# A gMLP layer's norm applied behind its projections, gate chains between the small steps of its mixing, and two weight units split earlier at each border

## The chip, the cores and the metric

The kernel runs on one core of a Trainium2 chip. The metric is the device time of one launch in microseconds (us), the median of three runs. Five engines work side by side, each with its own instruction queue: TensorE (PE, with the weight loads shown apart as PEld), VectorE (DVE), ScalarE (ACT), GpSimd (POOL) and SyncE (SP), which here only issues DMAs. An engine waits for another at a semaphore. TensorE's clock is at one of two levels, 2.4 GHz (granted clock 1.00) or 1.2 GHz (0.50).

## The reference, cut to what matters

One inference step of a two-layer decoder for a prompt of 1024 tokens and a group of 8 samples of one token, with width 1024. Layer 0 mixes by two kinds of attention, layer 1 by a chunked gMLP; each mixer is followed by a SwiGLU FFN of width 2816. Only the second mixer's norm and what follows matter here:

```python
def rms_norm(x, g):
    y = xf * lax.rsqrt(jnp.mean(xf * xf, axis=-1, keepdims=True) + NORM_EPS)
    return (y * g).astype(x.dtype)

def chunk_gmlp(h, w_in, g_v, b_v, w_s, b_s, w_out):
    z = jax.nn.gelu(h @ w_in, approximate=False)
    u, v = z[..., :D_C], z[..., D_C:]
    v = layer_norm(v, g_v, b_v)
    return (u * chunk_mix(v, w_s, b_s).astype(u.dtype)) @ w_out, v
```

with `x += mixer(rms_norm(x)); x += swiglu(rms_norm(x))` in every layer. The factor of a token in `rms_norm` is one number for a whole row of `x`, so `(x*g*r) @ w` equals `r * ((x*g) @ w)`. `chunk_mix` multiplies each group of 128 channels by a causal 128x128 matrix over 128 positions.

## The kernel before

**Layout.** The activations lie transposed in SBUF: `xT`, 8 tiles `m` of 128 channels by 1032 tokens (8 samples, then the prompt). Tokens are worked in three blocks `b`: 0 of 392, 1 of 384, 2 of 256. Every product of float32 numbers is made of three products of rounded halves: `x = Xh + Xl`, `w = Wh + Wl`, and `Wh*Xh + Wh*Xl + Wl*Xh` add up in PSUM (`split_products`, line 510; `chain`, line 503). A **chain** is the 24 matmuls that give 128 outputs for one block; of 392, 384 and 256 columns.

**Weights** come as units of 128x1024. SP loads them in order into two raw buffers (`load_unit`), as the splits free them. POOL splits most: `Wh` at line 377, `Wl` at line 380 (`split_unit`, `split_ahead`); ACT can round one (`round_unit`, 389), with POOL making the rest (`remainder_unit`, 398). Six buffers hold split units, so unit n can be split once PE is done with unit n - 6 (`wait_released`).

**A norm** (`norm_*`, lines 426 to 500) has per block: squares on ACT (`sq`, 428), their sum over m on POOL (`acc_sq`, 436), the sum over channels by a matmul with ones on PE (`norm_total`, 443), a square root on ACT (451), a reciprocal on DVE (457), then per m: `hs = xT*gain*acc_sq` on DVE (465), `Xh` rounded from it on ACT (472), `Xl = hs - Xh` on DVE for even m and on POOL for odd m (479).

**The order** of each engine's work is written out by hand, one function per engine and stage:
- An output projection (`narrow_pe`, `residual_dve`, `residual_act`, `residual_pool`) computes 24 chains; DVE adds each to `xT` (1550). The norm of blocks 0 and 1 is made while the later chains run. The next FFN's gate chains follow: this is a **border**, and there are two, at 790 and at 1895 us. `residual_pool` splits the next units with `ahead`.
- An FFN (`ffn_pe`, `ffn_dve`, `ffn_act`, `ffn_pool`) runs 11 steps of 12 gate chains, `hide` (`hf`, 1766; `Hl`, 1768) and 24 down chains of 6 matmuls, added to `xT` at 1777. In the last step of the first FFN (`LAST_STEP`: gates of blocks 0 and 1, down chains of block 0, gates of block 2, down chains of blocks 1 and 2) the gMLP's norm is made between.
- gMLP (`gmlp_pe`, `gmlp_act`, `gmlp_dve`): first the V half, 18 tiles with tokens on the partitions, 24 matmuls of 512 columns each (`wide_products`, 539 to 541), in 6 PSUM banks, freed by ACT's gelu (1968). Then U chains 1 to 6, while ACT and DVE make the layer norm of V (1977 to 2019); three small steps for the 8 samples (transposes 1940, DVE, 16 small matmuls 1944, copies 2036); the mixing of 16 half tiles (1952, DVE 2042); U chains 7 to 24. U's gelu goes from PSUM to `ug` (1997), `y = mixed * ug` on DVE (2065), then `Xh` on ACT (1988), `Xl` on DVE (2052, `low`) for the output projection. The bank of a U chain is free with its gelu.

The gelu of V, before the change:

```python
act.wait_ge(G["v_ps"], q + 1)
act.activation(dst, ps[0:r, q % V_BANKS, :], ACT.Gelu, accum_out=vsum[0:r, tt, c:c + 1]).then_inc(G["v_gelu"], 1)
```

Of the kernel before, what the change touches and what calls it, by code (L numbers as in the profile page):

```python
# [13 lines left out]
P = 128  # L14
# [3 lines left out]
NS = 8  # L18
# [74 lines left out]
def build(nc, a):  # L93
    with ExitStack() as ctx:
# [107 lines left out]
        vst = place("vst", [P, 4, TT])  # L202
        w00 = place("w00", [P, KT])
# [204 lines left out]
        def wl(n):  # L408
            return Wl[n % SPL]


        norm_sem = {k: (sem(f"norm_{k}"), n) for k, n in (
            ("squared", NB * KT), ("summed", NB * KT), ("total", NB), ("root", NB), ("rstd", NB),
            ("scaled", NB * KT), ("high", NB * KT), ("low_dve", NB * KT // 2), ("low_pool", NB * KT // 2))}

        NORMS = [None] + [{k: Counted(x, n * j) for k, (x, n) in norm_sem.items()} for j in range(3)]
# [1167 lines left out]
        def residual_pool(pool, base, order, norm, ahead):  # L1584
# [10 lines left out]
            for b in range(NB):  # L1595
                if b == NB - 1:
                    ahead(base + HALF + SPL)
                    ahead(base + HALF + 1 + SPL)
# [30 lines left out]
        def ffn_pe(pe, f, base, norm, bank_free, after, between):  # L1629
            def step(i, is_last):  # L1630
# [10 lines left out]
                for p, (kind, x, y, half) in enumerate(jobs):  # L1641
# [707 lines left out]
```

## Time and profile before

| | us |
|---|---|
| median of 3 runs (2666.21 to 2667.39) | 2666.43 |
| the profiled execution, its own time | 2663.21 |
| its span, first to last instruction | 2661.4 |
| PE busy | 2580.7 |
| DVE, POOL, ACT busy | 1128.5, 1111.4, 545.6 |
| second FFN border, V tiles, mixing: about | 1895, 1562 to 1675, 1708 to 1730 |

How to read it: all durations come from the one profiled execution, and positions are us from the start of its span. "Idle before, releaser" is what ended an engine's wait. A busy engine is one that has an instruction under way, so an op that is held up while it runs looks long, not idle.

### The profile page before, as it was taken

What the parts mean: (1) busy time and instruction counts of PE and PEld (TensorE: products, weight loads), DVE (VectorE), ACT (ScalarE), POOL (GpSimd) and SP (SyncE); (2) the same over time, 40 slices, a digit from 0 to 9 for tenths busy, and PEclk for the clock granted to TensorE, in tenths of its full rate; (3) what the DMA queues carried; (4) which work ended last, traced back from release to release, by engine and by line L of the source; (5) the groups of instructions that cost most, each with busy time, mean ns of one, the idle gap of its engine ahead of it and who ended that gap; (6) DMA issues with size and microseconds to landing.
All of it is one profiled execution on the core that took longest, in us unless ns stands there. A gap on an engine that the chain in (4) does not pass through costs nothing.

```text
span 2661.4 us, 42811 instructions
## 1 busy us (share of the span) xinstructions
PE 2580.7 (97%) x16377; PEld 2351.9 (88%) x16377; DVE 1128.5 (42%) x2234; ACT 545.6 (21%) x1255; POOL 1111.4 (42%) x713
## 2 busy tenths in 40 slices
PE   7999989999999999999999999999999999999999
PEld 6777756656899999999999977899999999999999
DVE  6636537667344333333333360433733333333333
ACT  5201126666321000000000141321300000000001
POOL 4224115566666443333333363426643333334440
PEclk9999989999999999999999999999999999999999
DMA  5223147767312111111111111102011111111111
GB/s 160 66 78 89 56 130 233 217 204 211 90 32 80 45 43 47 47 41 46 47 47 47 32 40 40 49 21 60 26 60 43 47 47 47 47 47 47 47 32 64
DMA packets 218460, 189.85 MB, mean 71 GB/s; under 512 B 29443, under 2 KB 171523, under 8 KB 217956
## 3 DMA queue, kind: packets, MB, share of 16 engines
q1 hardware_dynamic: 200996, 161.89, 21.0%
q10 hardware_dynamic: 17344, 26.35, 2.7%
q8 instruction: 76, 1.25, 0.2%
q14 instruction: 44, 0.36, 0.0%
HBM read 171.19 MB, written 17.01 MB: 71 GB/s over the span
## 4 chain that ended last, share of the span: by engine, by line
PE 69%; DVE 2%; POOL 2%; ACT 1%; issue 1%; ACTq 0%; POOLq 0%; DVEq 0%
PE ps L506 64%; DVE hs L465 1%; PE ps L539 1%; PE ps L541 1%; PE ps L540 1%; PE ps L1952 1%; ACT ps L1977 1%; POOL acc_sq L436 1%; DVE acc_sq L457 0%; PE ps L1184 0%; POOL Xl L479 0%; DVE Xl L479 0%; PE ps L1165 0%; PE ps L1212 0%; POOL Wl L398 0%
## 5 line engine op out<-in xcount | busy, mean ns | idle before, releaser
L506 PE MATMUL ps<-Xh,Wh 128*128 128x256 f32 (+2 forms) x2712 | 872.5, 322 | 14.1 <-POOL Wl L380 7.3
L506 PE MATMUL ps<-Xl,Wh 128*128 128x256 f32 (+2 forms) x2712 | 867.2, 320 | 0.0
L506 PE MATMUL ps<-Xh,Wl 128*128 128x256 f32 (+2 forms) x2712 | 866.1, 319 | 0.0
L377 POOL TENSOR_TENSOR Wh<-raw,zeros 128x1024 fp32r<-128x1024 f32 x178 | 353.8, 1988 | 1075.0 <-PE ps L506 788.8
L506 PEld LDWEIGHTS ps<-Xh,Wh 128*128 128x128 f32 x2712 | 510.0, 188 | 20.8 <-issue 17.0
L506 PEld LDWEIGHTS ps<-Xl,Wh 128*128 128x128 f32 x2712 | 510.0, 188 | 0.8
L506 PEld LDWEIGHTS ps<-Xh,Wl 128*128 128x128 f32 x2712 | 510.5, 188 | 0.0
L380 POOL TENSOR_TENSOR Wl<-raw,Wh 128x1024 fp32r<-128x1024 f32 x178 | 439.6, 2470 | 14.0
L1768 DVE TENSOR_TENSOR Hl<-hf,Hh 128x392 fp32r<-128x392 f32 (+1 forms) x132 | 180.2, 1365 | 465.9 <-ACT Hh L1696 465.9
L506 PE MATMUL ps<-Hh,Wh 128*128 128x392 f32 (+2 forms) x1056 | 341.6, 323 | 2.4 <-DVE xT L1777 2.4
L506 PE MATMUL ps<-Hl,Wh 128*128 128x392 f32 (+2 forms) x1056 | 338.8, 321 | 0.0
L506 PE MATMUL ps<-Hh,Wl 128*128 128x392 f32 (+2 forms) x1056 | 337.5, 320 | 0.0
L1777 DVE TENSOR_TENSOR xT<-ps,xT 128x392 f32<-128x392 f32 (+2 forms) x528 | 262.9, 513 | 167.2 <-PE ps L506 164.2
L1688 ACT ACTIVATE sg<-ps 128x392 f32<-128x392 f32 (+1 forms) x132 | 60.5, 458 | 1068.6 <-PE ps L506 1068.5
L539 PE MATMUL ps<-Wh,Xh 128*128 128x512 f32 (+1 forms) x576 | 230.8, 401 | 15.1 <-ACT VM_EARLY L1968 3.7
L541 PE MATMUL ps<-Wh,Xl 128*128 128x512 f32 (+1 forms) x576 | 229.4, 398 | 0.0
L540 PE MATMUL ps<-Wl,Xh 128*128 128x512 f32 (+1 forms) x576 | 229.0, 397 | 0.0
L1766 DVE TENSOR_TENSOR hf<-ps,sg 128x392 f32<-128x392 f32 (+1 forms) x132 | 67.2, 509 | 326.2 <-PE ps L506 322.0
L506 PEld LDWEIGHTS ps<-Hh,Wh 128*128 128x128 f32 x1056 | 199.7, 189 | 3.3 <-DVE xT L1777 3.1
L506 PEld LDWEIGHTS ps<-Hl,Wh 128*128 128x128 f32 x1056 | 200.3, 190 | 0.0
L506 PEld LDWEIGHTS ps<-Hh,Wl 128*128 128x128 f32 x1056 | 200.2, 190 | 0.0
L1113 POOL TENSOR_TENSOR kring<-kring,qrep 128x512 f32<-128x512 f32 (+1 forms) x96 | 120.7, 1274 | 97.8 <-DMA qrep<-q_sample 66.3
(219 smaller groups left out, 2443.8 us busy)
## 6 DMA issues: line engine op xcount, KB each, us to landing
raw<-in_w_gate_up SPq DMA_DIRECT2D x88, 512.0 KB, 3.8
raw<-in_w_down SPq DMA_DIRECT2D x44, 512.0 KB, 3.5
kring<-in_cache_a_k SPq DMA_DIRECT2D x64, 256.0 KB, 3.9
ring<-in_cache_a_v SPq DMA_DIRECT2D x64, 256.0 KB, 3.2
raw<-in_w_in_even SPq DMA_DIRECT2D x20, 512.0 KB, 4.1
raw<-in_w_in_c SPq DMA_DIRECT2D x16, 512.0 KB, 3.8
xs<-in_x_prompt SPq DMA_DIRECT2D x8, 512.0 KB, 7.9
q_prompt<-zt ACTq DMA_DIRECT2D x16, 256.0 KB, 2.0
```

The lines of the kernel that those rows point to most:

```text
L377: pool.tensor_tensor(h[:, :], r[:, :], zeros[:, :].to_broadcast([P, 1024]), ALU.add).then_inc(split_high, 1)
L380: pool.tensor_tensor(l[:, :], r[:, :], h[:, :].bitcast(F32), ALU.subtract).then_inc(split_done, 1)
L436: pool.tensor_tensor(acc_sq[b][:, 0:n], sq[t % 2][:, 0:n], other, ALU.add).then_inc(s["summed"].sem, 1)
L506: ins = nc.tensor.matmul(out, w, x, start=(j == 0), stop=(j == len(pairs) - 1))
L539: nc.tensor.matmul(out, xh, h, start=(k == 0), stop=False)
L540: nc.tensor.matmul(out, xh, l, start=False, stop=False)
L541: last = nc.tensor.matmul(out, xl, h, start=False, stop=(k == KT - 1))
L1113: pool.tensor_tensor(keys, keys, qrep[0:r, g, :], ALU.mult).then_inc(prod_done, 1)
L1688: act.activation(sg[:, k % NB, 0:w], ps[:, gate_bank(i, is_last, k), 0:w], ACT.Silu).then_inc(f["silu"].sem, 1)
L1766: dve.tensor_tensor(hf[:, k % NB, 0:w], ps[:, bank, 0:w], sg[:, k % NB, 0:w], ALU.mult).then_inc(f["hid"].sem, 1)
L1768: dve.tensor_tensor(Hl[:, t, c0:c0 + w], hf[:, k % NB, 0:w], Hh[:, t, c0:c0 + w].bitcast(F32), ALU.subtract).then_inc(f["low"].sem, 1)
L1777: dve.tensor_tensor(x, ps[:, jobs.index(("dn", b, m, 0)) % 6, 0:w], x, ALU.add).then_inc(f["dn_add"].sem, 1)
```

## The change

1. **The gMLP's norm.** `Xh` is rounded from `xT*gain` (ACT, `gain_high`) and `Xl = xT*gain - Xh` (DVE, `gain_low`), with no factor of the token, so neither waits for a norm; `hs` is gone, and POOL makes no `Xl` here. The factor comes behind the projections: PE makes the sums over channels behind V tile 3, per token on the partitions too (`token_totals`); V's gelu takes it as its scale; a U chain is multiplied by it on DVE on the way from PSUM to `ug` (`scaled`), and the gelu runs in place. A U bank is free with `scaled`.
2. **Mixing.** U chain 7 stands between the transposes and the 16 small matmuls, U chain 8 between those and the mixing.
3. **Borders.** In `residual_pool` the splits of `base + 10` and `base + 11` stand behind the first and second square-add of block 2, not behind the last; `norm_total` of block 2 stands behind the third gate chain, not the second.
4. `acc_sq`, `VM_LATE`, `ug`, `vsT`, `msT` lie elsewhere in SBUF.

```diff
+        def gain_high(act, s, g, b, m):
+            c0, n = BLOCKS[b]
+            act.activation(Xh[:, m, c0:c0 + n], xT[:, m, c0:c0 + n], ACT.Copy, scale=gains[:, g, m:m + 1]).then_inc(s["high"].sem, 1)
+        def gain_low(dve, s, g, b, m):
+            c0, n = BLOCKS[b]
+            s["high"].wait(dve, KT * b + m + 1)
+            dve.scalar_tensor_tensor(Xl[:, m, c0:c0 + n], xT[:, m, c0:c0 + n], gains[:, g, m:m + 1],
+                                     Xh[:, m, c0:c0 + n].bitcast(F32), ALU.mult, ALU.subtract).then_inc(s["low_dve"].sem, 1)
...
                 if b == NB - 1:
-                    ahead(base + HALF + SPL)
-                    ahead(base + HALF + 1 + SPL)
                     norm_apply_pool(pool, norm, b)
...
                     add(j0 + j)
+                    if b == NB - 2 and j < 2:
+                        ahead(base + HALF + j + SPL)
...
-                    if is_first(i) and p == 1:
+                    if is_first(i) and p == 2:
                         norm_total(pe, norm, NB - 1, NB * KT)
-                    if after and is_last and p == len(BLOCK_GATES[0]) * 2 + KT:
-                        norm_total(pe, after, 0, KT)
...
                 for m in range(KT):
                     square(0, m)
+                    gain_high(act, after, g, 0, m)
+                round_unit(act, nxt)
                 silu(4)
-                norm_root(act, after, 0)
-                round_unit(act, nxt)
...
+                high(4)
+                round_unit(act, nxt + 1)
+                silu(5)
+                high(5)
                 for b in (1, 2):
-                    norm_root(act, after, b)
-                    norm_apply_act(act, after, b)
+                    for m in range(KT):
+                        square(b, m)
+                        gain_high(act, after, g, b, m)
+                        if b == 1 and m in (1, 3):
+                            round_unit(act, nxt + 2 + m // 2)
...
+                hide(4)
+                hide(5)
                 for b in (1, 2):
-                    norm_apply_dve(dve, after, g, b)
+                    for m in range(KT):
+                        add(b, m)
+                        if m > 0:
+                            gain_low(dve, after, g, b, m - 1)
+                    gain_low(dve, after, g, b, KT - 1)
...
+            block(0)
             remainder_unit(pool, nxt)
...
             remainder_unit(pool, nxt + 1)
+            block(1)
             remainder_unit(pool, nxt + 2)
             remainder_unit(pool, nxt + 3)
+            block(2)
...
+        def token_totals(pe, norm):
+            norm["summed"].wait(pe, NB * KT)
...
+            total(0)
+            for tt in range(TT):
+                r, b = token_rows(tt), (tt >= 4) + (tt >= 7)
+                t0 = token_columns(tt) - BLOCKS[b][0]
+                last = nc.tensor.matmul(ps[0:r, 6, TOKENS_AT + tt:TOKENS_AT + tt + 1], acc_sq[b][:, t0:t0 + r], ones[:, 0:1], start=True, stop=True)
+            last.then_inc(G["v_tokens"], 1)
+            total(1)
+            total(2)
...
-                positive_wait(pe, G["u_gelu"], j - 5)
+                positive_wait(pe, G["u_scaled"], j - 5)
...
             last.then_inc(G["vst_ps"], 1)
+            u_block(6)
...
             last.then_inc(G["vs_ps"], 1)
+            u_block(7)
...
-                    act.activation(dst, ps[0:r, q % V_BANKS, :], ACT.Gelu, accum_out=vsum[0:r, tt, c:c + 1]).then_inc(G["v_gelu"], 1)
+                    act.activation(dst, ps[0:r, q % V_BANKS, :], ACT.Gelu, scale=vrstd[0:r, tt:tt + 1],
+                                   accum_out=vsum[0:r, tt, c:c + 1]).then_inc(G["v_gelu"], 1)
...
+            def scaled(j):
...
+                b, m = ORDER_NARROW[j]
+                n = BLOCKS[b][1]
+                dve.wait_ge(G["u_ps"], j + 1)
+                positive_wait(dve, G["y_done"], j - 1)
+                dve.tensor_tensor(ug[j % 2][:, 0:n], ps[:, j % 6, 0:n], acc_sq[b][:, 0:n], ALU.mult).then_inc(G["u_scaled"], 1)
...
                         low(b - 1, m2)
+                scaled(j + 2)
```

POOL's order at a border, from the first square-add of block 2 of the second output projection, before (`Xl<-hs` is the norm, `Wh` and `Wl` a split):

```order
L436 TENSOR_TENSOR acc_sq2_81<-sq0_77,acc_sq2_81 128x256
L436 TENSOR_TENSOR acc_sq2_81<-sq1_78,acc_sq2_81 128x256
L479 TENSOR_TENSOR Xl_62<-hs1_85,Xh_61 128x384
L479 TENSOR_TENSOR Xl_62<-hs3_87,Xh_61 128x384
L436 TENSOR_TENSOR acc_sq2_81<-sq0_77,acc_sq2_81 128x256
L479 TENSOR_TENSOR Xl_62<-hs1_85,Xh_61 128x384
L479 TENSOR_TENSOR Xl_62<-hs3_87,Xh_61 128x384
L436 TENSOR_TENSOR acc_sq2_81<-sq1_78,acc_sq2_81 128x256
L377 TENSOR_TENSOR Wh5_70<-raw1_64,zeros_59 128x1024
L380 TENSOR_TENSOR Wl5_76<-raw1_64,Wh5_70 128x1024
```

and after:

```order
L444 TENSOR_TENSOR acc_sq2_79<-sq0_80,acc_sq2_79 128x256
L383 TENSOR_TENSOR Wh5_70<-raw1_64,zeros_59 128x1024
L386 TENSOR_TENSOR Wl5_76<-raw1_64,Wh5_70 128x1024
L444 TENSOR_TENSOR acc_sq2_79<-sq1_81,acc_sq2_79 128x256
L383 TENSOR_TENSOR Wh0_65<-raw0_63,zeros_59 128x1024
L386 TENSOR_TENSOR Wl0_71<-raw0_63,Wh0_65 128x1024
L503 TENSOR_TENSOR Xl_62<-hs1_85,Xh_61 128x384
L503 TENSOR_TENSOR Xl_62<-hs3_87,Xh_61 128x384
L444 TENSOR_TENSOR acc_sq2_79<-sq0_80,acc_sq2_79 128x256
L503 TENSOR_TENSOR Xl_62<-hs1_85,Xh_61 128x384
```

The first split now stands behind one square-add instead of four, ahead of the `Xl` ops of block 1.

DVE's order at the end of the mixing, before (line 2042 is the mixing, 2065 is `y`):

```order
L2042 SCALAR_TENSOR_TENSOR VM_LATE_123<-ps,gv_53,RT_134 128x128 x16
L2063 TENSOR_TENSOR msT_128<-msT_128,ug0_125 128x8
L2065 TENSOR_TENSOR VM_EARLY_129<-VM_EARLY_129,ug0_125 128x3x128
L2065 TENSOR_TENSOR VM_EARLY_129<-VM_EARLY_129,ug1_126 128x3x128
L2065 TENSOR_TENSOR VM_LATE_123<-VM_LATE_123,ug0_125 128x2x128
L2063 TENSOR_TENSOR msT_128<-msT_128,ug1_126 128x8
```

and after (2092 is the mixing, 2115 is `y`, 2057 is `scaled`):

```order
L2092 SCALAR_TENSOR_TENSOR VM_LATE_123<-ps,gv_53,RT_134 128x128 x16
L2113 TENSOR_TENSOR msT_129<-msT_129,ug0_126 128x8
L2115 TENSOR_TENSOR VM_EARLY_125<-VM_EARLY_125,ug0_126 128x3x128
L2057 TENSOR_TENSOR ug0_126<-ps,acc_sq2_79 128x256
L2115 TENSOR_TENSOR VM_EARLY_125<-VM_EARLY_125,ug1_127 128x3x128
L2057 TENSOR_TENSOR ug1_127<-ps,acc_sq0_77 128x392
L2115 TENSOR_TENSOR VM_LATE_123<-VM_LATE_123,ug0_126 128x2x128
L2057 TENSOR_TENSOR ug0_126<-ps,acc_sq1_78 128x384
L2113 TENSOR_TENSOR msT_129<-msT_129,ug1_127 128x8
```

Between one `y` and the next now stands the `scaled` of the chain two later.

DVE's order in the last step of the first FFN, from the adds of block 0, before:

```order
L1777 TENSOR_TENSOR xT_60<-ps,xT_60 128x392 x8
L457 RECIPROCAL acc_sq0_79<-root0_82 128x392
L465 SCALAR_TENSOR_TENSOR hs0_84<-xT_60,gains_52,acc_sq0_79 128x392
L465 SCALAR_TENSOR_TENSOR hs1_85<-xT_60,gains_52,acc_sq0_79 128x392
L1766 TENSOR_TENSOR hf_122<-ps,sg_121 128x256
L1768 TENSOR_TENSOR Hl_120<-hf_122,Hh_119 128x256
```

and after, from the last two adds of block 0 (1788) with their `gain_low` (491):

```order
L1788 TENSOR_TENSOR xT_60<-ps,xT_60 128x392
L491 SCALAR_TENSOR_TENSOR Xl_62<-xT_60,gains_52,Xh_61 128x392
L1788 TENSOR_TENSOR xT_60<-ps,xT_60 128x392
L491 SCALAR_TENSOR_TENSOR Xl_62<-xT_60,gains_52,Xh_61 128x392 x2
L1777 TENSOR_TENSOR hf_122<-ps,sg_121 128x256
L1779 TENSOR_TENSOR Hl_120<-hf_122,Hh_119 128x256
L1777 TENSOR_TENSOR hf_122<-ps,sg_121 128x256
L1779 TENSOR_TENSOR Hl_120<-hf_122,Hh_119 128x256
```

The reciprocal and the `hs` ops are gone from this place, and one `gain_low` stands behind each add.

## Rows read from the trace of the kernel before

**Rows 1.** The page: its first part, and PE's granted clock in 40 slices.
```profile
PE 2580.7 (97%) x16377; PEld 2351.9 (88%) x16377; DVE 1128.5 (42%) x2234; ACT 545.6 (21%) x1255; POOL 1111.4 (42%) x713
...
PEclk9999989999999999999999999999999999999999
```

**Rows 2.** Waits of PE over the run: waiter, releaser, total us, times, longest.
```profile
PE ps L506 <- POOL Wl L380: 7.3, 2, 3.7
```

**Rows 3.** Waits of PE between 1500 and 1740 us, same columns.
```profile
PE ps L539 <- ACT VM_EARLY L1968: 3.7, 1, 3.7
PE ps L506 <- DVE xT L1777: 2.4, 1, 2.4
PE ps L443 <- POOL acc_sq L436: 2.1, 2, 1.4
PE ps L1940 <- DVE VM_LATE L2019: 1.9, 1, 1.9
PE ps L539 <- issue: 1.9, 1, 1.9
PE ps L1952 <- DVE vs L2036: 1.4, 1, 1.4
PE ps L1944 <- DVE vsT L2030: 1.2, 1, 1.2
```

**Rows 4.** Windows: stretch, its us, busy PE PEld DVE ACT POOL, PEclk, DMA share, GB/s.
```profile
803.00:811.00 8.00, 4.36 (x24) 4.22 (x24) 7.44 (x4) 1.31 (x3) 7.84 (x4) 1.00 0.21 66
1547.00:1563.00 16.00, 13.57 (x83) 12.85 (x82) 9.87 (x22) 5.10 (x11) 10.76 (x8) 0.89 0.26 81
1587.00:1593.00 6.00, 4.12 (x12) 2.81 (x11) 5.48 (x5) 1.30 (x3) 4.87 (x4) 0.73 0.00 1
1699.00:1709.00 10.00, 5.46 (x32) 3.61 (x31) 7.46 (x10) 2.16 (x3) 5.80 (x2) 0.67 0.00 0
1904.00:1912.00 8.00, 4.34 (x17) 4.22 (x17) 7.27 (x4) 1.31 (x3) 7.84 (x4) 0.79 0.21 66
```

**Rows 5.** Timeline of POOL at the second border: start us, us, operation, idle before.
```profile
1892.83 1.04 POOL L436 TENSOR_TENSOR acc_sq<-sq,acc_sq 128x256 f32<-128x256 f32 x1 [5.28 <-ACT sq L428]
...
1903.34 1.91 POOL L377 TENSOR_TENSOR Wh<-raw,zeros 128x1024 fp32r<-128x1024 f32 x1
1905.32 2.34 POOL L380 TENSOR_TENSOR Wl<-raw,Wh 128x1024 fp32r<-128x1024 f32 x1
```

**Rows 6.** Timeline of DVE in the last step of the first FFN.
```profile
1531.24 0.57 DVE L1777 TENSOR_TENSOR xT<-ps,xT 128x392 f32<-128x392 f32 x1 [0.50 <-PE ps L506]
...
1542.63 0.62 DVE L465 SCALAR_TENSOR_TENSOR hs<-xT,gains,acc_sq 128x392 f32<-128x392 f32 x1
```

**Rows 7.** Timeline of ACT: the gelus of the last two V tiles.
```profile
1669.87 0.60 ACT L1968 ACTIVATE VM_LATE<-ps 128x512 f32<-128x512 f32 x1 [4.87 <-PE ps L541]
...
1675.42 0.60 ACT L1968 ACTIVATE VM_LATE<-ps 128x512 f32<-128x512 f32 x1 [4.86 <-PE ps L541]
```

**Rows 8.** Chain that ended last, in time: U chains 9 to 11; nine projection chains.
```profile
1740.51 11.56 PE ps L506 x72
...
1799.40 37.07 PE ps L506 x216
```

**Rows 9.** Timeline of POOL: square-adds of block 0, last step of the first FFN.
```profile
1526.57 8.08 POOL L436 TENSOR_TENSOR acc_sq<-sq,acc_sq 128x392 f32<-128x392 f32 x7
```

**Rows 10.** Timeline of DVE while POOL splits weight units.
```profile
1703.40 2.39 DVE L2032 TENSOR_TENSOR msT<-vsT,w 128x64 f32<-128x64 f32 x1
...
1799.06 4.92 DVE L2052 TENSOR_TENSOR Xl<-VM_EARLY,Xh 128x384 fp32r<-128x384 f32 x2
```

**Rows 11.** Groups by form, 1500 to 1910 us: count, busy us, mean ns, idle before.
```profile
L1944 PE MATMUL ps<-ident,vsT 128*8 128x128 f32 x16 | 3.6, 419 | 1.2 <-DVE vsT L2030 1.2
```

**Rows 12.** Timeline of DVE in the mixing: first and last ops.
```profile
1710.62 1.13 DVE L2042 SCALAR_TENSOR_TENSOR VM_EARLY<-ps,gv,RT 128x128 f32<-128x128 f32 x4 [2.24 <-PE ps L1952]
...
1725.32 4.70 DVE L2042 SCALAR_TENSOR_TENSOR VM_LATE<-ps,gv,RT 128x128 f32<-128x128 f32 x16
```

More of the change, by code:

```diff
@@ L409, in wl @@
             return Wl[n % SPL]
+        ALL, EVEN, ODD = NB * KT, NB * KT // 2, NB * KT // 2
         norm_sem = {k: (sem(f"norm_{k}"), n) for k, n in (
-            ("squared", NB * KT), ("summed", NB * KT), ("total", NB), ("root", NB), ("rstd", NB),
-            ("scaled", NB * KT), ("high", NB * KT), ("low_dve", NB * KT // 2), ("low_pool", NB * KT // 2))}
-        NORMS = [None] + [{k: Counted(x, n * j) for k, (x, n) in norm_sem.items()} for j in range(3)]
+            ("squared", (ALL, ALL, ALL)), ("summed", (ALL, ALL, ALL)), ("total", (NB, NB, NB)), ("root", (NB, NB, NB)),
+            ("rstd", (NB, NB, NB)), ("scaled", (ALL, 0, ALL)), ("high", (ALL, ALL, ALL)),
+            ("low_dve", (EVEN, ALL, EVEN)), ("low_pool", (ODD, 0, ODD)))}
+        NORMS = [None] + [{k: Counted(x, sum(n[:j])) for k, (x, n) in norm_sem.items()} for j in range(3)]
         def norm_ready(eng, s, b):
@@ L1627, in build, with ffn_pe @@
         BY_BLOCK = [(t, b) for b in range(NB) for t in range(GF)]
-        def ffn_pe(pe, f, base, norm, bank_free, after, between):
+        def ffn_pe(pe, f, base, norm, bank_free, between):
             def step(i, is_last):
@@ L1791, in step @@
                     add(0, m)
-                if not after:
+                    if after and m > 0:
+                        gain_low(dve, after, g, 0, m - 1)
+                if after:
+                    gain_low(dve, after, g, 0, KT - 1)
+                else:
                     for k in range(4, HB):
@@ L1954, in gmlp_pe @@
                     last.then_inc(G["mix_ps"], 1)
-            for j in range(6, NB * KT):
+            for j in range(8, NB * KT):
                 u_block(j)
         def gmlp_act(act, norm):
-            norm_ready(act, norm, NB - 1)
+            gain_ready(act, norm, NB - 1)
             act.wait_ge(G["v_stat"], 1)
+            act.wait_ge(G["v_tokens"], 1)
+            act.activation(vroot[0:NS, 0:1], ps[0:NS, 6, TOKENS_AT:TOKENS_AT + 1], ACT.Sqrt, bias=eps[0:NS, 0:1], scale=1.0 / D).then_inc(G["v_root"], 1)
+            act.activation(vroot[:, 1:TT], ps[:, 6, TOKENS_AT + 1:TOKENS_AT + TT], ACT.Sqrt, bias=eps[:, 0:1], scale=1.0 / D).then_inc(G["v_root"], 1)
+            for b in range(NB):
+                n = BLOCKS[b][1]
+                norm["total"].wait(act, b + 1)
+                act.activation(acc_sq[b][:, 0:n], ps[:, TOTAL_BANK[b], 0:n], ACT.Sqrt, bias=eps[:, 0:1], scale=1.0 / D).then_inc(norm["root"].sem, 1)
+            act.wait_ge(G["v_rstd"], 2)
             for c in range(2):
@@ L2005, in gmlp_dve @@
             dve.memset(vsum[:, :, :], 0.0).then_inc(G["v_stat"], 1)
+            dve.wait_ge(G["v_root"], 2)
+            dve.reciprocal(vrstd[0:NS, 0:1], vroot[0:NS, 0:1]).then_inc(G["v_rstd"], 1)
+            dve.reciprocal(vrstd[:, 1:TT], vroot[:, 1:TT]).then_inc(G["v_rstd"], 1)
+            for b in range(NB):
+                norm["root"].wait(dve, b + 1)
+                dve.reciprocal(acc_sq[b][:, 0:BLOCKS[b][1]], acc_sq[b][:, 0:BLOCKS[b][1]]).then_inc(norm["rstd"].sem, 1)
             dve.wait_ge(G["v_gelu"], 2 * TT)
```

101 lines of the change are left out of this document (41 added, 60 removed).

## The prediction

> **What bounds the kernel now.** The page comes first. PE is busy for 2580.7 us of a 2661.4 us span, and the strip of its granted clock is at 9 in nearly every slice [rows 1]. No other engine is above 42%, so time can only come from PE's gaps and from matmuls run at the lower of its two clocks. The view of waits then names the gaps: 7.3 us in two waits of a gate chain for a weight remainder of POOL [rows 2], and between 1500 and 1740 us seven kinds of wait, 14.6 us together [rows 3]. The windows say what follows a gap: the mean granted clock is 0.89, 0.73, 0.67 and 0.79 in stretches that hold gaps of 2.4, 1.9, 1.9 and 3.7 us (1.00 is 2.4 GHz, the other level is 1.2 GHz), but 1.00 around the 3.7 us gap at 803 us [rows 4]. So half a clock follows most such gaps, not all. Its price: 0.79 over 8 us is 0.21 x 8 x 2 = 3.4 us at 1.2 GHz, which cost PE half, 1.7 us.
>
> Against all this the sum is made from the profiled execution: its own time is 2663.2 us, 3.2 us below the median of 2666.43 us, and I take the difference off that median.
>
> **A. Weight units at the borders.** At both borders POOL's order is the last square-add, then `Wh`, then `Wl` of the unit that the third gate chain needs [rows 5]; `Wl` ends 1907.66 and PE starts. The change puts these two units behind the first and second square-add of block 2. Their buffers are free once PE's chain behind that add is done, so both can be ready before PE asks. Gone: 7.3 us [rows 2] and the half clock behind the second border, 1.7 us [rows 4]. What is late next: POOL's last square-add, which ends just before 1903.3, moves back by the splits now ahead of it, 2 x (1.9 + 2.4) = 8.6 us, less the 5.3 us for which POOL idled there [rows 5], so to 1906.6 or later. PE asks for that sum in the third `norm_total`, moved from behind chain 2 to behind chain 3: PE was free at 1907.8 - 3.7 = 1904.1, with a total of 0.6 just done, so chain 3 of 4.3 us (B) now ends about 1907.8. Queued behind it are all further gate chains. Bounds: 0 and 3 us a border; I take 0.5 each, because the two times nearly meet. A = -7.3 - 1.7 + 1.0 = **-8.0 us**.
>
> **B. Last step of the first FFN and the V tiles.** Before, PE went from the end of the down chains of block 0 (their last add starts 1531.2 [rows 6]) to the last V tile (its gelu starts 1675.4 [rows 7]) in 144.3 us. I rebuild that stretch. A block-0 plus a block-1 chain of 24 matmuls take s, a block-2 chain c: s + c = 11.56 and 4s + c = 37.07 [rows 8], so s = 8.5, c = 3.0, or 2.8 without the drain behind it; a down chain of 6 matmuls is a quarter: 1.07, 1.05, 0.71. Four gates of block 2: 11.3. Sixteen down chains: 8.4 + 5.7. Eighteen V tiles of 5.55 (gelu starts 1669.87 and 1675.42 [rows 7]): 99.9. Three totals, 1.5, and the 0.3 between the two halves stay. Together 127.1 us.
> Now what is new.
> - `gain_low` on DVE: one op of 0.62 us, by the row of the old `hs` of the same form [rows 6], right behind each add. It reads two SBUF tensors, and so do POOL's square-adds, 7 in 8.08 us, 1.03 each with the hand-over [rows 9]. In this trace such ops take turns: two DVE ops of 0.55 took 4.92 us beside weight splits, and one of 64 columns 2.39 [rows 10]. So one step in m takes 1.03 + 0.62 = 1.65 us, where PE's down chains take 1.07, 1.05 and 0.71. Block 0's adds, from 1531.2 - 7 x 1.07 = 1524 on, then take 13 us and hold nobody up. The last gate ends 1531.1 + 11.3 = 1542.4 and its `hide` 1.2 later; ten steps of 1.65 on, at 1560.1, comes the third add of block 2, which the first V tile waits for. PE without stalls would be there at 1531.1 + 25.4 = 1556.5. Stall: 4.2 us (bounds 1.5, if DVE gets in without waiting, and 9, if each `gain_low` of block 2 sits through a 2.4 us split). Behind such gaps I take one stretch of half clock, 1.7.
> - The SBUF copy `Xh` with a scale operand costs ACT what the old copy did; ACT has slack. One table load each way leaves this stretch, beside other work: nothing.
> - `token_totals`: 9 fp32 matmuls of one column, two passes each, 18 instructions. The nearest row is the 16 small matmuls of `vs`, 3.6 us in all [rows 11] at half clock [rows 4], so 0.11 each at full: 2.0 us. Bounds 0.5 and 4.
>  The Trainium skill, "TensorE: Matmul & The Clock Gate", section "Wait — 56ns, not 53.3ns?", says that matmuls start no closer than about 25 ns however small they are; by that alone the 18 would cost 0.45 us and the total be 1.5 us lower. The rows here, at 0.11 with the weight load before each, decide.
> - The sums are complete well before V tile 2 ends, and the three later waits (1.4 for a sum, 1.9, 3.7 for the first gelu [rows 3]) go, since the gelu needs only PE's totals, two square roots and two reciprocals of 9 columns. The long reciprocals (2.6 each) lie beside 60 us of V tiles. V tile loads: SP fetches units 3 and 4 behind the splits of 1 and 2, which come no later than before. POOL's third and fourth remainder end about 1560 and 1562.5, needed 2.8 and 4.2 us into the first tile: just in time.
> B = 127.1 + 4.2 + 1.7 + 2.0 = 135.0; 135.0 - 144.3 = **-9.3 us**.
>
> **C. Mixing.** From the last V tile to the start of chain 9 of U, 1740.5 [rows 8] less its own 3.0 and 0.3 behind it, it is 61.8 us. Unchanged: 27 us up to the `vs` transposes, the 1.9 us wait for `v_norm` included. Then a U chain of 4.3 stands where PE waited 1.2, the 16 small matmuls run at full clock, 1.9, a chain of 4.2 where it waited 1.4. The mixing is paced by DVE: its first op starts 1710.6 and its last ends 1730.0, 19.4 us, plus 1.1 for the first half tile [rows 12]. New: chain 9 waits until bank 2 is free, which is no longer ACT's gelu, long done, but DVE's `scaled(2)`. That stands behind the last mixing op and `y(0)`: 0.17 + 0.55 + 0.42 and hand-offs, 1.3 us after DVE's end, a PE gap of 2.4 us with everything queued behind. Sum 27 + 4.3 + 1.9 + 4.2 + 19.4 + 1.1 + 1.3 = 59.2, that is -2.6. Two gaps (1.9 and 2.4) can each bring a half clock of 1.7; I take one. C = **-0.9 us**. From there on DVE spends about 0.6 us more in each 4 us chain, hidden.
>
> **D. Start of the output projection.** `y(j)` now runs one chain later than before, so the last `y` and the four `low` ops of block 0 meet POOL's four back-to-back splits, and each waits for its turn of 2.4 us [rows 10]. Five turns are 12 us from the end of chain 21 of U; PE reaches the projection after three chains, 9.9 (3.0 and 0.3 each). If ops of 8 columns need no turn, it is hidden. Bounds 0 and 2.1 + 1.7; I take **+2.0 us**.
>
> Sum: -8.0 - 9.3 - 0.9 + 2.0 = -16.2; 2666.4 - 16.2 = **2650 us**.
>
> **The rivals.**
> 1. *The port is milder and no clock falls.* B's stall 1.5, no half clock, D at 0: 2650 - 2.7 - 1.7 - 1.7 - 2.0 = 2642. For it: the gap at 803 us brought no half clock [rows 4]. Against: four others did.
> 2. *Gains handed back as waits.* `norm_total` waits 3 us a border with a half clock (+8), D at its upper bound (+2): 2660. For it: POOL's order at the border now carries 8.6 us more ahead of the last sum.
> 3. *The borders don't gain at all*, because the split is still released late, by the buffer or by the load of the raw unit: 2658. Against: the raw unit is two splits old by then.
> 4. *DVE turns set the last step, and the kernel is slower.* If each `gain_low` waits through a weight op, not a square-add, one m takes 0.57 + 2.46 = 3.0 us and more [rows 10]. The first V tile waits for the 19th add, 1524 + 19 x pace. At 3.1 that is 1583, 22 us later than I take, and the time 2672. It decides from a pace of 3.1; at 2.8 the change is even. Against: POOL has only eight weight ops there.
>  The Trainium skill, "SBUF — State Buffer", section "SBUF: two separate sides", speaks against the change in the same way: a DVE op with two SBUF inputs and a GpSimd op that reads SBUF take an exclusive lock for the whole instruction. By that rule, the trace agrees [rows 10].
>
> **Chances.** Forecast 0.52, rival 1 0.18, rival 2 0.15, rival 3 0.08, rival 4 0.03, and 0.04 for a small net effect by several of these. A measurement of this kernel can tell about 0.2%, 5.3 us. Faster by more: 0.91; within: 0.06; slower by more: 0.03. The range reaches from rival 1 to the middle of 2 and 3: 2641 to 2659.
>
> **What would show it.** Right: no wait of L506 for `Wl` at the borders; no wait for gelu or a sum among the V tiles; a PE wait of 1 to 4 us for an `xT` add before the first V tile; one of about 2.4 us for `ug` at chain 9; 18 small matmuls in about 2 us; PE's last V tile some 17 us earlier than now. Wrong: `norm_total` waiting over 2 us at a border; DVE steps over 2 us apart in the last step; a clock below 1 in other stretches; the projection waiting over 4 us for `Xl`.

## The result: 2639.1 us, 11 us under the forecast and 2 us under its range

| | median, us | executions | range |
|---|---|---|---|
| before | 2666.32 | 4 | 2665.62 to 2667.39 |
| changed | 2639.13 | 4 | 2636.49 to 2640.30 |

The ratio is 0.9898, with a 95% interval of 0.9886 to 0.9911. The sign was right, the size was not: 2650 was forecast, with a range of 2641 to 2659. The medians of this document leave out two single executions, 3148.7 us of `total_early` and 2989.2 us of `norm_only`, whose mean granted clocks were 0.75 and 0.79. The profiled executions differ less than the medians: 2663.21 and 2640.03 us, spans 2661.4 and 2638.2, so 23.2 us. That pair can be split by stage with the same instructions of both traces as marks (start times, us from the start of each span):

| mark | before | changed | stage took | change |
|---|---|---|---|---|
| DVE, 16th add of the first output projection | 763.10 | 761.59 | | -1.5 (no changed code) |
| DVE, 6th `hf` of the first FFN | 843.95 | 838.76 | 80.85, 77.17 | -3.7 first border |
| DVE, 61st `hf` | 1497.29 | 1492.14 | 653.34, 653.38 | 0.0 |
| DVE, first op after the last V tile | 1676.14 | 1659.47 | 178.85, 167.33 | -11.5 last step and V tiles |
| PE, start of the second projection | 1799.40 | 1781.30 | 123.26, 121.83 | -1.4 mixing, U, start of the projection |
| DVE, 16th add of the second projection | 1863.89 | 1845.80 | 64.49, 64.50 | 0.0 |
| DVE, 6th `hf` of the second FFN | 1946.14 | 1922.98 | 82.25, 77.18 | -5.1 second border |
| end | 2661.4 | 2638.2 | 715.3, 715.2 | 0.0 |

The page of the changed kernel, its first part and PE's clock in 40 slices, beside [rows 1]:

```profile
PE 2570.8 (97%) x16395; PEld 2346.3 (89%) x16395; DVE 1130.3 (43%) x2248; ACT 545.2 (21%) x1255; POOL 1100.0 (42%) x701
...
PEclk9999999999999999999999999999999999999999
```

PE has 18 more matmuls and yet is busy for 10 us less: that is the clock. (The slice at 8 in [rows 1] is gone too, but it covers 333 to 399 us, where the code is the same.) Next the waits of PE in the changed kernel (waiter, releaser, total us, times, longest), which answer to [rows 2, 3]:

```profile
PE ps L530 <- DVE ug L2057: 2.7, 2, 2.4
...
PE ps L1964 <- DVE VM_LATE L2069: 1.8, 1, 1.8
...
PE ps L530 <- DVE xT L1788: 1.2, 1, 1.2
...
PE ps L563 <- DVE Xl L491: 0.9, 1, 0.9
```

No wait for a weight remainder at a border is left, and none for a gelu or a square-add among the V tiles. The waits shown come to 6.6 us; those of [rows 2, 3] to 21.9. The windows of the changed kernel (columns as in [rows 4]), around the last adds before the V tiles, the transposes, and the mixing with its 2.4 us gap behind it:

```profile
1550.00:1560.00 10.00, 7.89 (x40) 6.54 (x40) 7.97 (x13) 4.58 (x12) 9.43 (x8) 1.00 0.36 107
1684.00:1692.00 8.00, 7.19 (x38) 6.82 (x39) 4.45 (x6) 0.00 (x0) 4.88 (x2) 0.79 0.00 0
1697.00:1721.00 24.00, 20.07 (x151) 18.08 (x150) 20.38 (x73) 1.03 (x3) 0.00 (x0) 1.00 0.14 40
```

Between 870 us and the last few us this execution holds a single stretch at 1.2 GHz, behind the wait for `v_norm` (the wait of L1964 above; 0.79 over 8 us). The execution before held seven such stretches of 3.4 us in the same part, 1.7 us of delay each.

**A border.** POOL at the second border of the changed kernel (start, us, operation), which answers to [rows 5], and then PE's total:

```profile
1869.94 1.89 POOL L383 TENSOR_TENSOR Wh<-raw,zeros 128x1024 fp32r<-128x1024 f32 x1
1871.91 2.39 POOL L386 TENSOR_TENSOR Wl<-raw,Wh 128x1024 fp32r<-128x1024 f32 x1
1875.66 1.04 POOL L444 TENSOR_TENSOR acc_sq<-sq,acc_sq 128x256 f32<-128x256 f32 x1 [1.36 <-ACT sq L436]
1876.65 2.22 POOL L383 TENSOR_TENSOR Wh<-raw,zeros 128x1024 fp32r<-128x1024 f32 x1
1878.95 2.59 POOL L386 TENSOR_TENSOR Wl<-raw,Wh 128x1024 fp32r<-128x1024 f32 x1
...
1889.01 0.73 POOL L444 TENSOR_TENSOR acc_sq<-sq,acc_sq 128x256 f32<-128x256 f32 x1
```

```profile
1889.80 0.70 PE L451 MATMUL ps<-acc_sq,ones 128*128 128x256 f32 x2
```

The first unit is split at 1874.3, some 11 us before the third gate chain, which needs it, starts. The last sum ends at 1889.74, that chain 0.07 us before it. "The two times nearly meet" was right, and the wait is nothing.

### The profile page after: what moved, and what is told of

It reads as the page before. It is cut to its first block, busy times and chain, and to the rows that moved or that the text cites. A ratio compares the mean times of both kernels' runs of the same rounds, so it can differ in the third digit from the quotient of the medians.

```text
span 2638.2 us, 42844 instructions
## 1 busy us (share of the span) xinstructions
PE 2570.8 (97%) x16395; PEld 2346.3 (89%) x16395; DVE 1130.3 (43%) x2248; ACT 545.2 (21%) x1255; POOL 1100.0 (42%) x701
## 4 chain that ended last, share of the span: by engine, by line
PE 69%; DVE 2%; POOL 2%; ACT 1%; issue 1%; ACTq 0%; POOLq 0%; DVEq 0%; PEldq 0%
PE ps L530 63%; PE ps L563 1%; PE ps L565 1%; PE ps L564 1%; ACT ps L2012 1%; POOL Xl L503 1%; POOL Wl L386 1%; POOL Wh L383 1%; DVE hs L473 0%; PE ps L1208 0%; PE ps L1978 0%; POOL acc_sq L444 0%; PE ps L1236 0%; PE ps L1189 0%; PE ps L2140 0%
```

## The experiments

Each kernel was timed against the kernel before on the same chip, in three sessions, each on another chip. All 33 executions of the kernel before in them have a median of 2663.3 us (2659.2 to 2667.6). The changed kernel's own median was 2638.5 and 2640.7 in the first and third session. Medians in us; "the stage" is one between the marks above.

| kernel | median | ratio to before, 95% |
|---|---|---|
| same_again | 2638.48 | 0.9896 to 0.9924 |
| old_border | 2651.82 | 0.9945 to 0.9970 |
| border_only | 2653.13 | 0.9950 to 0.9976 |
| total_early | 2650.57 | 0.9943 to 0.9969 |
| steps_together | 2637.97 | 0.9889 to 0.9917 |
| low_twice | 2653.27 | 0.9952 to 0.9976 |
| early_y | 2636.73 | 0.9887 to 0.9915 |
| shift_y | 2633.56 | 0.9879 to 0.9909 |
| same_third | 2640.67 | 0.9895 to 0.9924 |
| shift_again | 2633.68 | 0.9876 to 0.9905 |
| norm_only | 2651.87 | 0.9942 to 0.9968 |
| low_and_copy | 2647.34 | 0.9926 to 0.9952 |

**Executions** (`same_again`). The changed kernel again, unedited.

> The changed kernel once more, beside the kernel before. The two profiled executions differ by 23.2 us of span, the medians by 27.2 us. Theory 'executions': the missing 4 us lie in which execution was profiled: a kernel's executions differ by how many stretches of half clock they hold, 1.7 us each; then the medians here are again 25 to 29 us apart, the profiled pair lies inside the spread of the single times, and executions with a lower mean clock are the longer ones. Rival 'profile': the profiler itself takes time from one kernel and not from the other; then the profiled pair is again 4 us closer than the medians, whatever the clocks.

The medians were 24.9 us apart, 0.1 under the lower bound, and the profiled execution, 2638.99, is 24.2 below the profiled one of before: no 4 us closer than the medians, so the rival is out. The kernel before, in its 33 executions, took 2666.1 us on average at a mean granted clock of 0.987 (4 executions), 2663.6 at 0.989 (13), and 2661.5 at 0.991 (6). So executions do differ by their clock, by about 1.1 us for 0.001. That is less than the theory's price: one stretch of 3.4 us at half clock lowers the mean over 2640 us by 0.00065, so at 1.7 us each 0.001 would be 2.6 us (an estimate). Many stretches must cost less than the full 1.7. And the first four of the kernel before (2665.6 to 2667.4) lay near the slow end of that. Some 3 of the 11 us by which the forecast missed are of this kind: taken from 2663.3, the same sum would have given 2647. The three sessions in which the changed kernel stood beside the kernel before give 27.2, 24.9 and 23.0 us.

The third session repeated it once more:

> The changed kernel, on one chip with the three kernels below. As measured before: 2636 to 2642, and 24 to 27 us below the kernel before.

It gave 2640.67 (2636.5 to 2642.5), inside its window, and 23.0 below; the lower bound named was 24.

**The old border in the changed kernel** (`old_border`).

```diff
                 if b == NB - 1:
+                    ahead(base + HALF + SPL)
+                    ahead(base + HALF + 1 + SPL)
                     norm_apply_pool(pool, norm, b)
...
-                    if b == NB - 2 and j < 2:
-                        ahead(base + HALF + j + SPL)
...
-                    if is_first(i) and p == 2:
+                    if is_first(i) and p == 1:
```

> The changed kernel with the border of before (both splits behind the last square-add, the total behind the second gate chain). Theory 'waits and their clock': two waits of 3.7 us for the weight remainder come back, and a stretch of half clock behind none, one or both of them: +7.3 to +10.7, 2646 to 2650. Rival 'less': the waits come back shorter, because something else at the border gained; under 2644.

13.3 us more than `same_again`, over the upper bound. The waits are as expected:

```profile
PE ps L530 <- POOL Wl L386: 7.6, 3, 3.7
```

But its execution had one stretch of half clock behind the first wait and two behind the second, not two at most. The stages between the marks took 82.6 and 83.1 us, against 77.2 and 77.2: 11.3 us together.

**The new border in the kernel before** (`border_only`), the same edit the other way round.

> The kernel before with the change's border alone. Theory 'waits and their clock': 2666.3 - 7.3 to - 10.7, so 2656 to 2659, and no wait over 0.5 us for the total or a weight at either border. Rival 'only together': the border gains only in the changed kernel, 2662 or more.

2653.13, that is 10.2 below the kernel before on the same chip. The marks say 77.2 and 76.7 us for its two borders. Read against 2666.3, as it was written, the time lies under the window of 2656 to 2659; as a difference it is at the upper end of the 7.3 to 10.7. The two longest waits for a sum come to 0.8 us in the whole run, so the named bound of 0.5 each was passed by one, 0.7 us, which is the first sum of the gMLP's norm and no border. "Only together" is refuted.

**The splits early, the total not moved** (`total_early`). Only the line `p == 2` goes back to `p == 1`.

> The changed kernel with the splits early, but the total of block 2 behind the second gate chain as before. Theory 'the two moves belong together': POOL's last square-add ends about 805.5 with the splits ahead of it, PE asks after two chains, about 801.3, and waits 4.2 us at each border, with a half clock behind some of these: +8.4 to +11.8, 2647 to 2651, no better than with the old border. Rival 'POOL has room': the last sum is done by 802 to 803 as before; PE waits 1 us a border, 2641.

2650.57, in the window as a time and 12.1 above `same_again`, 0.3 over it as a difference; the old border took 2651.82. PE's waits:

```profile
PE ps L451 <- POOL acc_sq L444: 8.7, 2, 4.3
```

Twice 4.3 us, as worked out (4.2). Half of the border's change is worth nothing: the splits delay the sum by just what PE gains on the weights. With `norm_total` one chain later, as in the changed kernel, it is a gain. The other half alone, the total later with the splits late, was not run.

**The U chains back behind the mixing** (`steps_together`).

```diff
-            u_block(6)
...
-            u_block(7)
...
-            for j in range(8, NB * KT):
+            for j in range(6, NB * KT):
                 u_block(j)
```

> The changed kernel with U chains 7 and 8 back behind the mixing. Waits: 1.2 and 1.4 us come back between the small steps, and the 2.4 us behind the mixing go, because chain 9 then comes 8.5 us later: +0.2 us. Theory 'the chains bought clock, not waits': the small matmuls and the gaps around them bring stretches of half clock back, three of them before: +0.2 + 1.7 to + 0.2 + 5.1, 2641 to 2644.5. Rival 'waits alone': 2639.3 and no further half clock.

2637.97, so "waits alone": 1.2 and 1.4 us came back between the steps, the 2.4 behind the mixing went, and no stretch of half clock was added (one, behind the `v_norm` wait, as in the changed kernel). That is this execution: in the one of `norm_only` below, with the same order, 10.2 us at half clock stand behind that wait, as in the kernel before, and the stage took 138.7 us. The stage from the V tiles to the projection's first add took 137.2 us against 137.2 in `same_again`. Part 2 of the change does nothing that these medians show: its two chains fill two gaps and open one as large.

**Part 1 alone** (`norm_only`): the edits of `old_border` and `steps_together` together.

> The changed kernel with the border of before and with U chains 7 and 8 behind the mixing: part 1 of the change alone. Theory 'parts add up': the border is worth 10 to 13 us and the chains between the small steps nothing, so this stands 10 to 13 us above the changed kernel, 2649 to 2652, and 12 to 14 us below the kernel before. Rival 'the parts need each other': outside of that, because a stretch of half clock in one place moves those that follow.

2651.87, or 11.2 above the changed kernel and 11.8 below the kernel before. The first lies inside its window, the second 0.2 below it. So the parts add up: about 12 us for the norm, 10 to 13 for the border, nothing for the chains between the small steps. The other places in SBUF (part 4) are in this kernel too; no run has the norm without them.

**The low halves' differences computed twice** (`low_twice`).

```diff
         def gain_low(dve, s, g, b, m):
             c0, n = BLOCKS[b]
             s["high"].wait(dve, KT * b + m + 1)
+            u = KT * b + m
+            if u >= NH:
+                s["low_dve"].wait(dve, u - NH + 1)
+            dve.scalar_tensor_tensor(hs[u % NH][:, 0:n], xT[:, m, c0:c0 + n], gains[:, g, m:m + 1],
+                                     Xh[:, m, c0:c0 + n].bitcast(F32), ALU.mult, ALU.subtract)
```

> The changed kernel with the difference of each low half computed twice, the first time into an unused buffer. In the changed kernel a step of the last FFN step takes 1.32 us: 0.77 of POOL's add and 0.55 of DVE's op. Theory 'one after the other': the two engines' two-tensor ops share one turn and each costs only its own time, so a step is 1.32 + 0.57 = 1.9 us; block 1 ends 3.4 us later, the first V tile starts some 4 us later, and a half clock may follow: +4 to +6, 2643 to 2645. Rival 'a turn per op': each DVE op waits for a whole square-add and hand-over of 1.03, as in my prediction; a step of 2.7 us or more, +10 or more. Rival 'no turns': DVE and POOL run side by side; a step is DVE's own 0.55 + 0.57 + 0.57 = 1.7, +2.

2653.27: 14.8 above `same_again`, and 15.3 above `steps_together`, the nearest kernel of its own session. The stage of the last step and the V tiles took 182.3 us against 167.4. First what a step is in the changed kernel (timeline of DVE, then of POOL):

```profile
1524.26 0.55 DVE L1788 TENSOR_TENSOR xT<-ps,xT 128x392 f32<-128x392 f32 x1
1524.74 0.92 DVE L491 SCALAR_TENSOR_TENSOR Xl<-xT,gains,Xh 128x392 fp32r<-128x392 f32 x1
1525.58 0.55 DVE L1788 TENSOR_TENSOR xT<-ps,xT 128x392 f32<-128x392 f32 x1
```

```profile
1524.15 1.08 POOL L444 TENSOR_TENSOR acc_sq<-sq,acc_sq 128x392 f32<-128x392 f32 x1 [0.23 <-ACT sq L436]
1525.46 1.09 POOL L444 TENSOR_TENSOR acc_sq<-sq,acc_sq 128x392 f32<-128x392 f32 x1 [0.23 <-ACT sq L436]
```

1.32 us from add to add, where I had said 1.65. The add has one operand in PSUM and is not held (0.55, inside the square-add). The difference, 0.6 us where nothing holds it, takes 0.92 and ends 0.43 behind the square-add, at 1525.66; the next square-add has then been under way for 0.20, and is only 0.06 longer than the 1.03 of a free one. 1.09 + 0.43 - 0.20 = 1.32: the turns overlap at both ends. No row shows the 0.77 and 0.55 of the expectation. With the op twice:

```profile
1524.71 0.55 DVE L1793 TENSOR_TENSOR xT<-ps,xT 128x392 f32<-128x392 f32 x1
1525.18 0.92 DVE L494 SCALAR_TENSOR_TENSOR hs<-xT,gains,Xh 128x392 f32<-128x392 f32 x1
1526.03 1.40 DVE L496 SCALAR_TENSOR_TENSOR Xl<-xT,gains,Xh 128x392 fp32r<-128x392 f32 x1
1527.35 0.55 DVE L1793 TENSOR_TENSOR xT<-ps,xT 128x392 f32<-128x392 f32 x1
1527.83 0.61 DVE L494 SCALAR_TENSOR_TENSOR hs<-xT,gains,Xh 128x392 f32<-128x392 f32 x1
1528.36 0.61 DVE L496 SCALAR_TENSOR_TENSOR Xl<-xT,gains,Xh 128x392 fp32r<-128x392 f32 x1
1528.90 0.55 DVE L1793 TENSOR_TENSOR xT<-ps,xT 128x392 f32<-128x392 f32 x1
...
1559.49 2.69 DVE L494 SCALAR_TENSOR_TENSOR hs<-xT,gains,Xh 128x384 f32<-128x384 f32 x1
1562.11 2.69 DVE L496 SCALAR_TENSOR_TENSOR Xl<-xT,gains,Xh 128x384 fp32r<-128x384 f32 x1
```

Steps of 2.64 and 1.55 us in turn, 2.1 on average: in the long one each of the two ops meets a square-add (0.92 and 1.40), in the short one both are free (0.61), while POOL idles for 1.5 us until ACT has the next square. None of the three theories had that (1.9; 2.7 or more; 1.7). By the pace alone "one after the other" is nearest, but the time is that of "a turn per op". PE waits 10.2 us for adds here, where it waited 2.1. Of these, 4.2 are the slower pace, in five waits up to 1556 us. The other 6.0 come from the last two rows: the steps of block 1 now end after POOL has started its two weight remainders of 2.6 us, and each of two DVE ops sits through one. PE's clock is at half for 20 us, from 1549.7 on: it fell behind waits of 1.3 and 0.5 us, before the long one. Two windows of this kernel (columns as in [rows 4]):

```profile
1550.00:1556.00 6.00, 3.88 (x16) 3.12 (x14) 6.00 (x10) 3.39 (x7) 3.31 (x3) 0.50 0.00 0
1556.00:1564.00 8.00, 3.17 (x12) 2.71 (x12) 8.00 (x7) 2.05 (x4) 7.18 (x4) 0.50 0.12 32
```

This is my rival 4 at work, at two thirds of its 22 us, and from a pace of 2.1 on instead of 3.1: the remainders behind each block, which the slower pace runs into, gave more of the wait than the pace itself. In the changed kernel the last difference of block 1 gets in just before the remainders (timeline of DVE, then of POOL):

```profile
1549.85 1.01 DVE L491 SCALAR_TENSOR_TENSOR Xl<-xT,gains,Xh 128x384 fp32r<-128x384 f32 x1 [0.27 <-ACT Xh L485]
...
1552.08 1.31 DVE L491 SCALAR_TENSOR_TENSOR Xl<-xT,gains,Xh 128x256 fp32r<-128x256 f32 x1 [0.56 <-ACT Xh L485]
...
1553.64 2.27 DVE L491 SCALAR_TENSOR_TENSOR Xl<-xT,gains,Xh 128x256 fp32r<-128x256 f32 x1
```

```profile
1549.39 1.06 POOL L444 TENSOR_TENSOR acc_sq<-sq,acc_sq 128x384 f32<-128x384 f32 x1 [0.22 <-ACT sq L436]
1550.41 5.22 POOL L404 TENSOR_TENSOR Wl<-raw,Wh 128x1024 fp32r<-128x1024 f32 x2
```

PE's wait of 1.2 us ends with the first add of block 2, which stands behind that last difference. Beside the remainders lie only the first two differences of block 2, 1.3 and 2.3 us long for 0.5 of work. The first holds up the third add, and PE starts the first V tile 0.1 us behind that, after 0.9 us of waiting; the second holds up nobody.

**An extra op with one SBUF operand** (`low_and_copy`) in place of the doubled one.

```diff
+            dve.tensor_scalar(hs[u % NH][:, 0:n], xT[:, m, c0:c0 + n], gains[:, g, m:m + 1], None, ALU.mult)
```

> As the kernel that computed each difference twice, but the extra op has one SBUF operand (a product of xT with the gain, into the unused buffer) and no second one. With two SBUF operands it cost 14 us: steps of 1.55 and 2.63 us in turn, three ops held for 2.7 to 2.8 us by POOL's remainders, 20 us of half clock. Theory 'two operands take turns': an op with one SBUF operand is not held; a step is 1.32 us and its own 0.3 to 0.4, 1.7 us, the V tiles start 2 to 3 us later, +2 to +4.5 with a half clock, 2641 to 2643. Rival 'DVE's order': any further op of DVE between the others costs the same turn, +10 or more, 2649 or more.

2647.34, 6.7 above the changed kernel of the same session; the stage took 175.4 against 167.3. Both theories fail. The step is the 1.65 us that the first one gave, but the op is held all the same (timelines of DVE and POOL):

```profile
1522.83 0.41 DVE L494 TENSOR_SCALAR hs<-xT,gains 128x392 f32<-128x392 f32 x1
...
1524.18 0.72 DVE L494 TENSOR_SCALAR hs<-xT,gains 128x392 f32<-128x392 f32 x1
...
1531.98 1.18 DVE L494 TENSOR_SCALAR hs<-xT,gains 128x392 f32<-128x392 f32 x1
1533.08 2.75 DVE L495 SCALAR_TENSOR_TENSOR Xl<-xT,gains,Xh 128x392 fp32r<-128x392 f32 x1
```

```profile
1523.56 1.12 POOL L444 TENSOR_TENSOR acc_sq<-sq,acc_sq 128x392 f32<-128x392 f32 x1 [1.55 <-ACT sq L436]
...
1532.98 2.43 POOL L404 TENSOR_TENSOR Wl<-raw,Wh 128x1024 fp32r<-128x1024 f32 x1
```

Its 0.41 us become 0.72 when it starts inside a square-add of POOL (until 1524.68), and 1.18 inside another. The same section of the Trainium skill that the prediction used ("SBUF — State Buffer", "SBUF: two separate sides") names a second kind of DVE op that takes the lock, one in a two-port performance mode; these rows agree with that, though no row here shows in which mode an op ran. Two SBUF operands are not the only condition. The rest of the time is again the remainders: one last difference takes 2.75 us, the other 2.69, and PE waits 4.2 us for one add.

**The product y(0) inside the mixing** (`early_y`). On DVE, behind the tenth half tile:

```diff
                                                  gv[:, g:g + 1], RT[:, g, :], ALU.mult, ALU.add).then_inc(G["mix_done"], 1)
+                if tile == 4:
+                    dve.wait_ge(G["mix_done"], 8 * 3)
+                    gated(0)
+                    scaled(2)
```

Here `gated(j)` is the product with `ug`, taken out of the loop over j, which then makes products and `scaled` from j = 1 on.

> The changed kernel with the first product y(0), which needs only the first three token tiles, and the scaling of the third U chain moved from behind the mixing to behind its tenth half tile on DVE. Theory 'release': the bank for U chain 9 is free early, its wait of 2.4 us goes, and the mixing, paced by DVE, ends 1.1 to 1.2 us later: -1.2, 2637.9. Rival 'DVE sets the end anyway': the projection's start or a later wait takes it back, 2639 to 2640.

2636.73. The ratio, 0.9901, cannot be told from that of `steps_together`, 0.9903, and there was no changed kernel in that session, so the median decides nothing between -1.2 and nothing. The trace shows the mechanism: the wait for `ug` is gone from the list, waits of the mixing for DVE went from 1.3 to 2.1 us, the stage took 135.3 us where `same_again` has 137.2, so 1.9 less where 1.2 was worked out.

**U chain 7 ahead of the transposes** (`shift_y`), with the edit of `early_y`.

```diff
-            for j in range(6):
+            for j in range(7):
                 u_block(j)
...
-            u_block(6)
+            u_block(7)
...
-            u_block(7)
```

> As the one before, and U chain 7 moved ahead of the small transposes, chain 8 between these and the small matmuls, none behind those. Theory: the wait of 1.8 us for v_norm goes with the one half clock behind it (1.7), and a wait of 1.4 us for the copies of the small matmuls' output comes: -2.1, with the product early -3.3, 2635.8. Rival 'the gate follows the small steps': the new wait brings its own half clock, -1.6, 2637.5.

2633.56; its executions ran from 2630.7 to 2639.2 and so could be either. The repeat beside the changed kernel:

> The last variant once more (y(0) inside the mixing, U chain 7 ahead of the transposes), now beside the changed kernel on the same chip. Theory: two waits less and their half clock, 3 to 5 us below the changed kernel. Rival 'the session': the 2633.6 came from executions that happened to hold few stretches of half clock; then 0 to 2 us below it.

2633.68 (2632.8 to 2635.4) against 2640.67: 7.0 us less, more than either theory had; "the session" is out. Its window at the transposes, beside the 0.79 above, and its new wait:

```profile
1684.00:1692.00 8.00, 6.76 (x48) 5.93 (x47) 2.12 (x6) 0.00 (x0) 1.03 (x1) 1.00 0.01 2
```

```profile
PE ps L1977 <- DVE vs L2085: 1.4, 1, 1.4
```

The 1.4 us wait brought no half clock. The stage from the V tiles to the projection's first add took 133.9 us, 3.3 less than in `same_again`, as worked out, and 4.7 less than in `same_third`, which had a further stretch of half clock behind its wait for `ug`. The rest of the 9.7 us between these two profiled executions, 5.0 us, lies before the first border, in code that is the same; both hold 20.5 us at half clock there, so counting stretches does not explain it. This is the fastest kernel of the study. The ratio to before is 0.9891, the changed kernel's 0.9910 in the same session; the intervals overlap, so that it beats the changed kernel rests on the four executions of each in that session, which do not overlap, and on the stage's 3.3 us.

## Why the prediction was wrong, by its own steps

Against the profiled pair, the sum was -16.2 and the measured difference -23.2. The 11 us of the miss are 0.8 from A, 2.2 from B, 2.5 from C and D, 1.5 from before the first border, 3.2 from the base, and 0.9 by which the changed kernel's profiled execution lies above its median.

- **A, the borders: -8.0, measured -8.8 in the pair** and 10 to 13 in the medians of the runs that undo or isolate it. The waits were right to 0.1 us. The 1.0 for the total was nothing. The mis-sized term is the clock: I gave one stretch of half clock to the two waits, since the execution shown had none at 803 us [rows 4]. Both other kernels with these waits (`old_border`, `norm_only`) show one stretch at the first border and two at the second. One execution was taken for the rule.
- **B, last step and V tiles: -9.3, measured -11.5.** This is the step whose mechanism failed. "One step in m takes 1.03 + 0.62 = 1.65" is wrong: it lays two whole durations end to end, and the measured step is 1.32, because the difference needs only 0.43 us behind the square-add and the next square-add starts 0.20 before its end. The 1.03 is not "with the hand-over" either. It is POOL's own time, and seven of them with 0.14 between two make the 8.08 of [rows 9]; in the kernel before a square-add with DVE idle takes as long (timeline of POOL, 1532.5 to 1533.4 us):

```profile
1532.47 1.03 POOL L436 TENSOR_TENSOR acc_sq<-sq,acc_sq 128x392 f32<-128x392 f32 x1
```

 PE waited 1.2 and 0.9 us, not 4.2, and no half clock followed (1.00 in the window above), where I had taken 1.7. Against this gain of 3.8 us over the forecast stands 1.5 us by which the rebuilt stretch of 127.1 was too short. The totals per token cost what was said (timeline of PE):

```profile
1571.32 2.07 PE L1920 MATMUL ps<-ones,acc_sq 128*8 128x1 f32 x18
```

 2.07 us for 18, 0.115 each, against 2.0 by the row and 0.45, an estimate, by the least distance between matmuls in the Trainium skill's "TensorE: Matmul & The Clock Gate" ("Wait — 56ns, not 53.3ns?"). Each of these has a weight load of its own before it, of which that distance says nothing; the row decided rightly.
- **C and D, mixing to projection: -0.9 and +2.0, measured -1.7 and +0.3**, from the last V tile's gelu to the start of U chain 9 (1737.22 us before, 1718.81 in the changed kernel) and from there on. (The first of [rows 8] is chains 10 to 12, not 9 to 11; the working used it as such.) This gain is clock and not code. From the first op after the V tiles to the second projection the kernel before took 123.3 us with three stretches of half clock, but 121.7 with one, in `border_only`, whose code is the same there; the changed kernel took 121.8 and 121.7 with one, 123.1 with two. The wait for `scaled(2)` was 2.4 us, as worked out to the tenth, and the one half clock came, behind `v_norm`. D did not come: that is the other term that was wrong. I counted five turns of 2.4 us behind chain 21. There were three (timeline of DVE), the last low half of block 0 was done at 1778.64, and PE came to the projection 2.2 us later:

```profile
1771.53 2.10 DVE L2115 TENSOR_TENSOR VM_EARLY<-VM_EARLY,ug 128x384 f32<-128x384 f32 x1
1773.56 2.36 DVE L2101 TENSOR_TENSOR Xl<-msT,Xh 128x8 fp32r<-128x8 f32 x1
1775.85 0.55 DVE L2102 TENSOR_TENSOR Xl<-VM_EARLY,Xh 128x384 fp32r<-128x384 f32 x1
1776.32 1.85 DVE L2101 TENSOR_TENSOR Xl<-msT,Xh 128x8 fp32r<-128x8 f32 x1
1778.09 0.55 DVE L2102 TENSOR_TENSOR Xl<-VM_EARLY,Xh 128x384 fp32r<-128x384 f32 x1
```

 Between two ops of POOL DVE fits more than one op: an op of 8 columns waits for the turn like any other, and the next, of 384, goes in behind it in the same turn.
- **Before the first border: 0, measured -1.5**, with the same code. This execution holds two stretches less there, six against eight, which may be the cause; the pair of `same_third` and `shift_again` shows that their count does not settle it.
- **The base: 2666.4.** In three later sessions the kernel before took 2663.3. I had seen that the profiled execution was 3.2 us under the median and took the median.

Of the rivals, the first (milder port, no half clock, 2642) was the nearest, with 0.18. The range ended at its time, though the rival kept A's clock at one stretch and my base had 3 us to give; it took in the bounds of the costs and not the spread of the executions, 8 us for the kernel before.

## What to carry to other kernels

A wait of PE of 2 to 4 us costs its own length and, here more often than not, one or two stretches at half clock of up to 1.7 us each; price it from several executions, since one trace can show none. When two engines take turns on SBUF, the pace is not the sum of two rows read alone, since the turns overlap at both ends (1.32 us here, not 1.65), and the cliff is where an op falls behind a long one (here a 2.6 us weight remainder). A gain in one stage of one pair of traces can be clock alone; look for an execution of the old code with as many stretches. Moving a producer earlier helps only with the consumer moved too: the early splits were worth nothing until the total stood one chain later.

## What the runs showed that I had not expected

- The same gap is followed by half clock in one execution and not in another. Behind the 2.4 us wait for `ug` the clock stayed at 1.00 in the changed kernel and fell in `same_third` (0.84 over the 8 us from 1715). Behind the 1.8 us wait for `v_norm` it fell in all three executions of the changed kernel, and not in `low_twice` or `low_and_copy`. What decides this stays open.
- A wait of 1.4 us on its own, in `shift_again`, was followed by none.
- A DVE op with one SBUF operand is held by POOL too: 0.41 us alone, 0.72 and 1.18 beside a square-add.
